# Hybrid decoder step on one core: the work ahead of the recurrence in smaller pieces, sample state products by head pairs, and decode lots in eight pieces of one form

## What is computed

```python
xn = rms_norm(x, ln1_g)
proj = [shift_prev, xn] @ w_in               # q, k, v, f of 8 FoX heads; r, k, v, wl, al, gl of 8 RWKV heads
logit[t, s] = q_t . k_s / 8 + c_q[t] - c_k[s]  # FoX attention; past keys and values of the samples: 32 pages
attn = softmax(logit) @ v                      # of 128 positions per sequence, found through a page table
for t:                                         # RWKV-7 recurrence, per head a 64 x 64 state S
    sa = S @ a_t
    S = S * w_t + sa b_t^T + v_t k_t^T
    y_t = S @ r_t
h = x + [attn, group_norm(y) ...] @ w_out
out = rms_norm(h + (silu(hn @ w_gate) * (hn @ w_up)) @ w_down)
```

## Time and profile before

| | us |
|---|---|
| median of 3 runs | 1510.46 (1509.58 to 1511.0) |
| profiled execution | 1510.73 |
| its span in the profile | 1509.0 |
| PE busy in the span | 1402.4 (93%) |
| DVE busy | 438.2 (29%) |
| ACT busy | 357.0 (24%) |
| mean granted TensorE clock | 0.969 |
| to the first key transposes | 335.6 |
| decode stage | 335 to 912 |
| projection and feed-forward | 912 to 1509 |

### The profile page before, as it was taken

The page is one execution under the profiler, slowest core; times in us unless marked ns, Lnnn a source line. Parts: engine busy times, 40 slices in busy tenths (PEclk is TensorE's granted clock), DMA queues, the critical chain, the costliest instruction groups (busy, mean ns, idle before and its releaser), DMA issues.

```text
span 1509.0 us, 27895 instructions
## 1 busy us (share of the span) xinstructions
PE 1402.4 (93%) x11595; PEld 953.3 (63%) x11595; DVE 438.2 (29%) x917; ACT 357.0 (24%) x713; POOL 110.0 (7%) x223
## 2 busy tenths in 40 slices
PE   5999999988799999999989779999999999999997
PEld 4755666655577777777755454477777777744442
DVE  5022355455844444444445241310000000000002
ACT  3010233245444343443433331100000000000011
POOL 6283000000000000001202010000000000000000
PEclk9999899998799999999989889999999999999998
DMA  5187011023898787878957897003111221150001
GB/s 206 57 189 205 7 57 35 1 75 110 284 312 277 229 292 247 294 255 266 272 191 261 315 314 245 1 13 100 56 56 56 89 79 56 56 195 0 0 0 63
DMA packets 123174, 219.32 MB, mean 145 GB/s; under 512 B 11451, under 2 KB 35078, under 8 KB 123046
## 3 DMA queue, kind: packets, MB, share of 16 engines
q1 hardware_dynamic: 115154, 193.64, 38.3%
q0 software_dynamic: 7824, 23.85, 5.9%
q10 hardware_dynamic: 68, 0.02, 0.0%
HBM read 203.06 MB, written 14.41 MB: 144 GB/s over the span
## 4 chain that ended last, share of the span: by engine, by line
PE 84%; DVE 5%; DMA 4%; ACT 3%; issue 2%; SPq 1%; POOL 0%; DVEq 0%; POOLq 0%; ACTq 0%
PE PS L1369 23%; PE PS L736 13%; PE PS L1388 10%; PE PS L1178 6%; PE PS L1192 4%; PE PS L1308 4%; PE PS L1237 4%; PE PS L709 2%; DMA arena<-in_cache_k 2%; DMA out_wkv_prompt<-arena 1%; PE PS L1394 1%; PE PS L992 1%; PE PS L1002 1%; PE PS L996 1%; ACT arena L1622 1%
## 5 line engine op out<-in xcount | busy, mean ns | idle before, releaser
L1369 PE MATMUL PS<-arena 128*128 128x288 f32 x1408 | 342.1, 405 | 1.2 <-DVE arena L2251 1.2
L1369 PEld LDWEIGHTS PS<-arena 128*128 128x128 f32 x1408 | 265.7, 189 | 77.4 <-DVE arena L2251 1.4
L736 PE MATMUL PS<-arena 128*128 128x301 f32 (+1 forms) x736 | 197.7, 426 | 0.0
L1622 ACT ACTIVATE arena<-PS 128x512 f32<-128x512 f32 x256 | 141.4, 596 | 192.8 <-PE PS L1178 192.4
L1178 PE MATMUL PS<-arena 128*128 128x128 f32 x1024 | 153.8, 296 | 27.1 <-DMA arena<-in_cache_k 15.1
L736 PEld LDWEIGHTS PS<-arena 128*128 128x128 f32 (+1 forms) x736 | 136.6, 189 | 54.7 <-issue 13.6
L1178 PEld LDWEIGHTS PS<-arena 128*128 128x128 f32 x1024 | 122.1, 151 | 55.8 <-issue 24.2
L1388 PE MATMUL PS<-arena 128*128 128x512 f32 x352 | 151.5, 592 | 1.5 <-DVE arena L2277 1.5
L1388 PEld LDWEIGHTS PS<-arena 128*128 128x128 f32 x352 | 66.5, 189 | 86.2 <-issue 84.3
L2277 DVE TENSOR_TENSOR arena<-PS,arena 128x576 f32<-128x576 f32 x22 | 16.7, 758 | 327.0 <-ACT arena L1686 327.0
L1686 ACT ACTIVATE arena<-PS 128x576 f32<-128x576 f32 x22 | 14.3, 651 | 329.8 <-PE PS L1369 329.8
(11 more groups left out here) (360 smaller groups left out, 1409.9 us busy)
## 6 DMA issues: line engine op xcount, KB each, us to landing
arena<-in_cache_k SPq DMA_DIRECT2D x256, 256.0 KB, 4.3
arena<-in_cache_v SPq DMA_DIRECT2D x256, 256.0 KB, 4.8
arena<-in_w_gate SPq DMA_DIRECT2D x11, 1024.0 KB
arena<-in_w_up SPq DMA_DIRECT2D x11, 1024.0 KB
arena<-in_w_in SPq DMA_DIRECT2D x5, 2048.0 KB, 11.9
forgets_after<-arena POOLq DMA_DIRECT2D x64, 128.0 KB, 8.5
arena<-forgets_after SPq DMA_DIRECT2D x32, 256.0 KB, 5.1
arena<-in_w_down SPq DMA_DIRECT2D x4, 2048.0 KB
```

The lines of the kernel that those rows point to most:

```text
L736: ins = mm(PS[0:width, bank, 0:HALF], wring[:, c % 2, k, c0:c0 + width], xnT[:, k, half * HALF:(half + 1) * HALF], start=(k == 0), stop=(k ...
L1369: ins = mm(PS[:, 4 * (f % 2) + 2 * w + half, 0:HO], fring[r % FR][:, c:c + P], hT[:, k, half * HO:(half + 1) * HO], start=(k == 0), stop=( ...
L1622: av(KTs[:, (2 * i + q) % LOT], PS[:, T_USE[("k", L, i, q)] % 2, :].rearrange("p (g n) -> p g n", g=NG), ACT.Copy)\
```

## The change

It does four things.

1. `N_PRE` is 32 instead of 17, and `rwkv_pre` has 32 steps on each engine. On DVE nine operations are cut in two, and each has a step to itself. `rwkv_due` reads a table: one step after each piece from the first on up to the 32 steps ahead of the recurrence (two after piece 0), then the other 123 steps at an even rate to piece 245, where an even piece gets a step only if the count is one behind. So most steps stand after odd pieces.
2. The pieces of a lot on PE become K0 | S3 of the lot before | K1 | S0 | K2 T | S1 | K3 | S2 V0 to V3. The product of one column is gone; `add_output` waits for `v_free` of the last value product. The other engines' generators follow, and the uses of the two banks are listed anew. The last lot's S3 and `add_scores` come after the loop.
3. SP asks for all four key pages of a lot ahead of the four value pages of the lot before.
4. In `sample_states` the four products of a head pair are ordered K of both heads, B of both heads, after one wait for both heads' masked copies.

```diff
-        N_PRE = 17
+        N_PRE = 32
...
+        RWKV_DUE = []
+        for piece in range(8 * LOTS):
+            done = RWKV_DUE[-1] if piece else 0
+            if piece < N_PRE - 1:
+                done = piece + 2
+            else:
+                aim = N_PRE + 1 + (piece - N_PRE + 2) * (N_RWKV - N_PRE - 1) / (8 * LOTS - 10 - N_PRE)
+                done += done < aim if piece % 2 else done < aim - 1
+            RWKV_DUE.append(min(N_RWKV, done))
...
         def rwkv_due(piece):
-            return min(N_RWKV, 1 + piece * (N_RWKV - 1) // (8 * LOTS - 20))
+            return RWKV_DUE[piece]
...
-                for i in range(3):
+                for i in range(LOT):
                     key_page(pr, j, numbers, i)
                 if vj is not None:
-                    for i in range(2):
-                        value_page(vpr, vj, value_numbers, i)
-                key_page(pr, j, numbers, 3)
-                if vj is not None:
-                    for i in range(2, LOT):
+                    for i in range(LOT):
                         value_page(vpr, vj, value_numbers, i)
...
-                        pe.wait_ge(S["um_ready"], h + 1)
...
-                        mm(o, nat_[64:P, K_, hc], Um[64:P, h % 2, 1].rearrange("p b i -> p (b i)"), start=True, stop=False)
-                        ins = mm(o, nat_[64:P, B_, hc], Um[64:P, h % 2, 0].rearrange("p b i -> p (b i)"), start=False, stop=True)
...
+                    pe.wait_ge(S["um_ready"], 2 * g + 2)
...
+                    for w, u in ((K_, 1), (B_, 0)):
+                        for hp in range(2):
...
-                if half:
-                    mm(PS[:, OUT, 511:512], ident, ones[:, 0:1], start=False, stop=True, skip_group_check=True).then_inc(S["ov_ready"], 1)
...
                     turn_keys(L, 0)
                     yield
+                    if L:
+                        page_scores(L - 1, 3)
...
+                    yield
                     turn_keys(L, 1)
+                    yield
                     page_scores(L, 0)
                     yield
+                    turn_keys(L, 2)
                     if L:
                         turn_probs(L - 1)
                     yield
-                    turn_keys(L, 2)
                     page_scores(L, 1)
                     yield
...
                     turn_keys(L, 3)
+                    yield
                     page_scores(L, 2)
-                    yield
                     if L:
-                        lot_values(L - 1, 1)
-                    yield
-                    page_scores(L, 3)
+                        lot_values(L - 1)
...
-                ch.wait()
-                ch(tt(Bd, Bd, Kd, ALU.mult))
-                yield
+                for p in pair:
+                    ch.wait()
+                    ch(tt(Bd[:, p], Bd[:, p], Kd[:, p], ALU.mult))
+                    yield
...
-                dve.wait_ge(S["ov_ready"], L + L // NLOT + 2)
+                dve.wait_ge(S["v_free"], LOT * (L + 2))
```

194 lines of the change are left out of this document (109 added, 85 removed).

## The result

The changed kernel takes 1534.85 us (1532.92 to 1538.4) where the kernel before takes 1510.47: a ratio of 1.0165, interval 1.0143 to 1.0187. It is 24 us slower where 23 us faster was forecast, and lies outside the range. Its profiled execution spans 1534.7 us at a mean granted clock of 0.952; that of before spans 1509.0 at 0.969.

The account below looks back on a forecast made before the run. In the decode stage's middle PE's own time and short waits were taken as the bound. The terms -9.9 - 1 + 1.3 - 9 - 2 - 3 = -23.6, rounded to -23, took 1510.7 to 1488 us; range 1472 to 1505.

Parts of the forecast that it names:

- (a): Lots: the one-column product goes 32 times at 0.31 us of PE, -9.9 us, bound -9 to -10.
- (b): PE's order: neighbouring groups with different array tiles fall from 476 to 412, -1 us, bounds -3 to +2.
- The rival that gave -11 for them: Every form change saved is worth 0.17 us on top, -11 us, giving 1477 us; chance 0.11.
- (c): Lots: PE's waits for DVE's copy, ACT's exponential and key page behind key page go, -17.8 us.
- (d): Lots: turned weights wait 0.54 us behind page 2's keys in 28 lots, +15.1; DVE's longer block, +4.
- (e): Start, 335 to 420 us: finer steps, shorter stops and a better clock make 85 us 76, -9, bounds -19 and -3.
- (f): Sample states: paired heads' products overlap on two column tiles, two of four groups win 0.9, -2 us, bounds -4 to +1.
- (g): End: recurrence steps move into lots where PE waited for cache keys, -3 us, bounds -8 to +4.
- (h): SP's order: all four key pages asked for ahead of the value pages of the lot before, taken at 0.
- the rival on the slow side: Cache data come late: PE waits 1.25 us for keys in each of 28 lots, +12, 1522 us; chance 0.08.

Follow-up runs that it names:

- b_O: The kernel before without the one-column product of each lot, DVE waiting for the last value product itself: 0.9957, 1506.8 us.
- a_T: The changed kernel with the turned weights one group later, behind the scores of page 1: 1.0075, 1525.5 us.
- a_start: The changed kernel with 8 and 8 thrown-away products at the two stops of the start (346 to 349 us): 1.0073, 1520.9 us.
- a_st3: The changed kernel with 3 and 3 thrown-away products at the two stops of the start: 1.0076, 1522.7 us.
- a_fill: The changed kernel with 16 thrown-away products ahead of each of the four paired groups of the sample states: 1.0085, 1526.0 us.
- b_S: The kernel before with only the sample states' products in pairs: ratio 1.0008.
- a_noS: The changed kernel with the sample states' products one head at a time again, each waiting for its own head's copies: 1.0140, 1532.6 us.
- a_noQ: The changed kernel with the loads in the old order (three key pages, two value pages, the fourth key page, two value pages): ratio 1.0153.
- b_OF: The kernel before without the one-column products, with 24 and 6 thrown-away products ahead of the second and third sample-state group: ratio 0.9958.

## Why the prediction was wrong, point by point

- **(a) One-column product, -9.9:** right in sign. b_O has -6.5, with an interval of -10.1 to -2.9.
- **(b) Form changes, -1:** too small to be told apart by any run. The rival that gave -11 for them is out by b_O, which saves 62 of them and gains 10.1 us at most where the rival needs 20. That does not refute the gap of 0.17 us itself. What the Trainium skill ("TensorEngine Tiling (Array Packing)", Tiling Modes) says of a drain would have given those 11 us; no run here shows them.
- **(c) Waits that go, -17.8:** too large by its source, as far as is known. For 420 to 750 us it has 4.5 and 3.3 us from the weight loads, and 4.9 from nine stops at 0.54. On PE's products the same three groups are 2.8, 2.5 (where the profile names the key copy and not the exponential) and 3.6 us, together 8.9 and not 12.7: the load side shows a stop longer than the product side does. Which of the two is what the kernel loses isn't shown. And the changed lots have stops of their own there that no term had: 3.1 us behind DVE (L2011), 2.2 behind L2148, 1.8 for keys, 2.7 with no releaser that the profile names.
- **(d) Waits that come, +15.1:** right in kind; in size as priced by one pair of traces (10.6 us for 21 lots against 11.3), and nearer half of it against the other runs. That the trace's total is 16.1 us is partly luck: it holds a stop of 4.66 us which the term didn't have and which a_T doesn't remove, and the ordinary ones are 0.40 us on the products, not 0.54.
- **(e) The start, -9:** the step that failed; measured, the changed kernel is 5.7 us later at the third lot. The term counted a better clock as a gain that follows when DVE's operations get smaller ("if half of the work in it runs at the upper one, PE gets back up to 8 us"). The waits at the start did shrink as said: the long one for lot 2's keys at 382 us is gone. But the clock is not a result of the sum of the waits. Two stops of 0.6 and 0.7 us at 346 to 349 us put 27 us of a fully busy PE to half speed, and a_start and a_st3 show that covering them gives back 12 to 14 us (1534.9 to 1522.7 and 1520.9). With them covered the third lot is 7.1 us ahead of the kernel before: the 9 us were nearly right for the waits, and the clock took them and more. The bounds of the term (-19 to -3) had no side on which the clock gets worse. Two rows had the warning: the 0.67 us stop at 350.99 in the earlier trace rows, and 0.81 in a stretch that is 82% busy.
- **(f) Sample states, -2:** the two column tiles do overlap (a group takes 1.94 us at the upper clock where the earlier trace rows has 2.94), as forecast. The price was missed: with both heads' copies awaited, each group stands where DVE has first to do something else that PE has just given it (turned weights, values or scores), a chain of 3.6 us at the second group. The prediction named the wait and let two of four groups win. All four lost, 12.2 us where the kernel before loses 3.4, and the lower clock behind them cost 7 to 12 more by a_fill. b_S shows that the same edit at the old places is neutral: so the placement is what matters more. a_noS, with the new places and without the pairs, gives back only 4 us.
- **(g) The end, -3:** the waits for cache data at the end are 11.7 us in the changed kernel (7.9 for values, 3.8 for keys) and were 10.7, 7.9 of them for keys: they moved from keys to values, and nothing was gained.
- **(h) Order of loads, 0:** right, by a_noQ.
- **The range.** Its upper end of 1505 came from terms that were each thought independent, and the rival on the slow side was about late data. None of the rivals had the clock on the losing side. The miss is 49 us in the profiled executions, 25.7 of loss and 23.6 of gain that didn't come. By the lag of the output's addition, and with the terms shared out over the lots (an estimate), 16 of it lie before the third lot, 6 between the third and the 24th, 18 between the 24th and the 26th, where the sample states are, and 9 behind. Of the first, a_start gives back 14, of the third, a_fill 7 to 12. The last 9, where (g) was to gain, no single experiment took apart. What single edits give back holds for this order only, since the falls of the clock can move, as b_OF shows.

## What to carry to other kernels

Cost a stop of PE twice: by its length, and by the work that stands behind it in the order, as if that ran at the lower clock, wherever the profile shows the clock falling at stops of that size. A change that moves steps about must be read in the order of both sides at once: ask for each wait of PE what the releasing engine has to do between the last thing that PE gave it and the release, and whether PE has that much work in between. Where such a stop can't be moved, thrown-away products of about its own length are a cheap test of whether the clock is the cause, and sometimes a mend; one place mended alone may only pass the fall on to the next.

## What the runs showed of the hardware that was not expected

- PE can stay at the lower of its two levels for 27 us while it is busy without a gap (busy 27.00 of 27.00 us, clock 0.50), after two stops of 0.60 and 0.69 us. With 0.94 us of thrown-away work in each, the same products ran at 1.00.
- The time of one and the same kernel goes with its mean granted clock: 8.3 us less between executions of a mean clock of 0.961 and 0.971. That is 0.5%: a difference of this size between two single executions can be nothing but this.
- Adding 15 us of products to an engine that was thought to be the bound made the kernel 9 us faster by the medians, 12 by the ratios (a_fill).
